# Gate and up as seven block products in three of four feed-forwards, with GpSimd making four weight sums and the low part of two weight blocks

## The chip, the cores and the metric

The kernel runs on one core of a Trainium2 chip. The metric is the device time in microseconds (us) of one execution, as a median over runs; less is better.

## The reference

A trunk of two layers over 512 tokens plus 16 learned meta tokens (L = 528 in all), model width 1024, float32. Each layer is a feed-forward, a mixer (layer 0: gated convolution and a state space; layer 1: windowed attention), and another feed-forward. Only the feed-forwards matter here:

```
def swiglu(x, w_gate, w_up, w_down):
    return (jax.nn.silu(x @ w_gate) * (x @ w_up)) @ w_down

h = h + FFN_RESIDUAL * swiglu(rmsnorm(h, norm_ff1[layer]), ff1_w_gate[layer], ff1_w_up[layer], ff1_w_down[layer])
```

`w_gate` and `w_up` are 1024 x 2816, `w_down` is 2816 x 1024. The first three feed-forwards work on 528 tokens, the last on the 512 real ones.

## The kernel before

Features lie on the 128 partitions, tokens along the free dimension. A float32 product is made as three TensorE passes: each operand is split into a high part (rounded to the fp32r type by ScalarE's copy) and a low part (what is left, by a VectorE subtraction), and the passes are high by high, high weight by low input, low weight by high input. 2816 is 22 blocks of 128.

**Gate and up.** One *unit* is one block of 128 columns of `w_gate` and of `w_up`, all eight blocks of the contraction: 16 weight blocks of 128 x 128, 2048 elements on each partition. SyncE loads a unit into one of two `raw` buffers (`load_unit`, L635), as soon as VectorE has finished the low part of the unit two before it. ScalarE makes `wh` (`split_high`, L1184), VectorE `wl` (`split_low`, L1464), both with two slots. TensorE's `x_job` makes the gate tile in PSUM banks 0 and 1 and the up tile in banks 2 and 3 (`mm3`, L729). For 528 tokens each pass is two matmuls of 264 columns; for the last feed-forward (`REAL`) it is one of 512. So a unit is 16 x 3 x 2 = 96 matmuls of 264 columns, or 48 of 512. VectorE scales the tiles out of PSUM by the norm `r` (`t_a` L1517, `t_c` L1520), ScalarE takes the silu (L1222), VectorE multiplies (L1523), ScalarE makes `act_h` (L1224), VectorE `act_l` (L1525).

**Down.** The 22 blocks of a feed-forward are done in two parts, 12 and 10 (`PART`). After each part eight down tiles follow (`down`), each a sum over the part's blocks: 72 or 60 matmuls. VectorE adds each to `h` (`residual`, L1500). In the last part the next norm's input is made tile by tile (`norm_input`).

Each engine has its own instruction stream in order, and semaphores order them. GpSimd makes state-space tables in the first feed-forward, issues their transfers in the mixer, makes attention's constants right after it, and has nothing at all to do in feed-forwards 1, 2 and 3 (they are counted from 0).

## Time and profile before

| | |
|---|---|
| median of 3 runs | 1954.45 us (1953.42 to 1957.58) |
| the profiled execution, its time | 1953.96 us |
| its span, first to last instruction | 1951.9 us |
| TensorE busy | 1931.4 us, 99% |
| VectorE busy | 967.5 us, 50% |
| ScalarE busy | 605.0 us, 31% |
| GpSimd busy | 315.3 us, 16% |
| mean granted TensorE clock | 0.994 of 2.4 GHz |

The profile gives for each engine its busy time, for groups of equal instructions their count and mean duration, and for a stretch of the timeline each instruction's start, its duration and, in brackets, the idle time before it and what ended it. PE is TensorE, DVE VectorE, ACT ScalarE, POOL GpSimd. Durations of matmuls overlap, so the cost of one is read from how many fit in a stretch.

### The profile page before, as it was taken

How to read it: one execution, taken by the hardware profiler on the slowest of the kernel's cores; microseconds unless marked ns; L12 is line 12 of the kernel's file. 1: busy time of each engine (PE TensorE's matmuls, PEld its weight loads, DVE VectorE, ACT ScalarE, POOL GpSimd, SP SyncE). 2: the span in 40 equal slices, each digit the busy share in tenths (PEclk: the TensorE clock that was granted, in tenths of full speed). 3: DMA queues.
4: the chain of work that ended last, by engine and by line, in shares of the span. 5: the costliest groups of instructions: out<-in, count | busy, mean ns of one | idle time of the engine just before them, and what ended most of it. 6: DMA issues, size and time to landing. Idle time of an engine off the chain costs nothing.

```text
span 1951.9 us, 33853 instructions
## 1 busy us (share of the span) xinstructions
PE 1931.4 (99%) x13943; PEld 1814.2 (93%) x13943; DVE 967.5 (50%) x1059; ACT 605.0 (31%) x710; POOL 315.3 (16%) x568
## 2 busy tenths in 40 slices
PE   7999999999999999999999999999999999999999
PEld 7999999999999999999999999999877778888887
DVE  5443377566665443344564433445555564433443
ACT  5222222332243222222332222223455332222222
POOL 2888888011130000000000000000011000000000
PEclk9999999999999999999999999999999899999999
DMA  6322544354333323432233323322311133233323
GB/s 176 87 81 82 151 134 151 125 128 129 99 84 87 86 82 88 110 87 70 81 108 88 93 83 102 87 70 81 108 44 44 44 104 90 76 96 108 98 71 90
DMA packets 329026, 185.61 MB, mean 95 GB/s; under 512 B 7288, under 2 KB 322968, under 8 KB 328952
## 3 DMA queue, kind: packets, MB, share of 16 engines
q1 hardware_dynamic: 323280, 166.81, 30.6%
q0 software_dynamic: 5344, 17.69, 3.2%
q8 instruction: 53, 0.87, 0.2%
q14 instruction: 21, 0.17, 0.0%
q10 hardware_dynamic: 328, 0.07, 0.0%
HBM read 173.56 MB, written 9.80 MB: 94 GB/s over the span
## 4 chain that ended last, share of the span: by engine, by line
PE 93%; DVE 3%; issue 2%; ACT 2%; ACTq 0%; POOL 0%; DVEq 0%
PE ps L729 77%; PE ps L948 5%; PE ps L990 2%; PE ps L1009 1%; PE ps L1045 1%; PE ps L1173 1%; PE ps L1141 1%; DVE wl L1464 1%; DVE arena L1845 0%; ACT arena L1410 0%; PE ps L770 0%; PE ps L883 0%; PE ps L909 0%; PE ps L908 0%; PE ps L899 0%
## 5 line engine op out<-in xcount | busy, mean ns | idle before, releaser
L729 PE MATMUL ps<-xl,wh 128*128 128x264 f32 (+1 forms) x2448 | 567.1, 301 | 0.0
L729 PE MATMUL ps<-xh,wh 128*128 128x264 f32 (+1 forms) x2448 | 566.1, 301 | 0.7 <-DVE t_a L1517 0.5
L729 PE MATMUL ps<-xh,wl 128*128 128x264 f32 (+1 forms) x2448 | 565.7, 301 | 0.0
L1464 DVE TENSOR_TENSOR wl<-raw,wh 128x2048 fp32r<-128x2048 f32 x173 | 412.8, 2386 | 168.6 <-ACT wh L1184 168.4
L729 PEld LDWEIGHTS ps<-xh,wh 128*128 128x128 f32 x2448 | 392.3, 188 | 18.0 <-DVE t_a L1517 1.1
L1184 ACT ACTIVATE wh<-raw 128x2048 fp32r<-128x2048 f32 x173 | 329.6, 1905 | 246.7 <-PE ps L729 211.2
L729 PEld LDWEIGHTS ps<-xl,wh 128*128 128x128 f32 x2448 | 391.2, 188 | 15.5 <-issue 0.2
L729 PEld LDWEIGHTS ps<-xh,wl 128*128 128x128 f32 x2448 | 391.1, 188 | 15.1
L729 PE MATMUL ps<-act_l,wh 128*128 128x264 f32 (+1 forms) x1232 | 284.7, 301 | 0.0
L729 PE MATMUL ps<-act_h,wh 128*128 128x264 f32 (+1 forms) x1232 | 284.6, 301 | 0.0
L729 PE MATMUL ps<-act_h,wl 128*128 128x264 f32 (+1 forms) x1232 | 284.3, 301 | 0.0
L1520 DVE TENSOR_TENSOR t_c<-ps,r 128x528 f32<-128x528 f32 (+1 forms) x88 | 61.9, 704 | 367.1 <-PE ps L729 367.0
L729 PEld LDWEIGHTS ps<-act_h,wh 128*128 128x128 f32 x1232 | 197.4, 188 | 7.7
L729 PEld LDWEIGHTS ps<-act_l,wh 128*128 128x128 f32 x1232 | 196.8, 188 | 7.4
L729 PEld LDWEIGHTS ps<-act_h,wl 128*128 128x128 f32 x1232 | 196.6, 188 | 7.5
L1224 ACT ACTIVATE act_h<-t_c 128x528 f32 (+3 forms) x88 | 56.5, 642 | 459.7 <-DVE t_c L1523 459.7
L310 POOL TENSOR_TENSOR arena<-arena 128x32 f32<-128x32 f32 (+7 forms) x245 | 186.2, 760 | 24.2 <-DMA ssm_tables<-arena 5.3
L613 POOL TENSOR_SCALAR arena<-arena 128x16 f32<-128x16 f32 x4 | 1.0, 259 | 902.4 <-DVE arena L1833 865.4
L1500 DVE SCALAR_TENSOR_TENSOR h<-ps,h 128x528 f32 (+2 forms) x72 | 50.7, 704 | 192.4 <-PE ps L729 184.2
L1222 ACT ACTIVATE t_bs<-t_a 128x528 f32<-128x528 f32 (+1 forms) x88 | 56.5, 642 | 285.1 <-DVE t_a L1517 285.1
L1525 DVE TENSOR_TENSOR act_l<-t_c,act_h 128x528 f32 (+3 forms) x88 | 70.6, 803 | 78.8 <-ACT act_h L1224 78.8
L1523 DVE TENSOR_TENSOR t_c<-t_c,t_bs 128x528 f32<-128x528 f32 (+1 forms) x88 | 71.0, 806 | 9.0
(296 smaller groups left out, 1686.8 us busy)
## 6 DMA issues: line engine op xcount, KB each, us to landing
raw<-in_ff_w_gate SPq DMA_DIRECT2D x88, 512.0 KB, 4.0
raw<-in_ff_w_up SPq DMA_DIRECT2D x88, 512.0 KB, 5.2
raw<-in_ff_w_down SPq DMA_DIRECT2D x64, 384.0 KB, 4.0
raw<-in_ff_w_down SPq DMA_DIRECT2D x64, 320.0 KB, 3.7
raw<-in_even_w_in SPq DMA_DIRECT2D x16, 512.0 KB, 5.2
raw<-in_attn_w_qkv SPq DMA_DIRECT2D x12, 512.0 KB, 4.6
raw<-in_even_w_out SPq DMA_DIRECT2D x8, 512.0 KB, 4.7
raw<-in_attn_w_o SPq DMA_DIRECT2D x8, 512.0 KB, 4.5
```

Of the source, the lines that this page charges most:

```text
L310: did(g.tensor_tensor(o, x, y, op))
L729: last = nc.tensor.matmul(ps[:, 2 * pair + hf, 0:nh], w[:, slot, b * P:(b + 1) * P], x[:, k0 + k, c0 + hf * nh:c0 + (hf + 1) * nh], start= ...
L948: last = nc.tensor.matmul(ps[:, 2 * (p % 2) + hf, 0:L // 2], w[:, slot, b * P:(b + 1) * P], x[:, k, hf * L // 2:(hf + 1) * L // 2], start= ...
L990: last = nc.tensor.matmul(ps[:, 2 * (d % 2) + hf, 0:L // 2], w[:, slot, b * P:(b + 1) * P], x[:, k, hf * L // 2:(hf + 1) * L // 2], start= ...
L1184: nc.scalar.activation(wh[:, c % 2, :], raw[:, c % 2, :], ACT.Copy).then_inc(wh_ready, 1)
L1222: nc.scalar.activation(t_b[:, cols], t_a[:, cols], ACT.Silu).then_inc(silu_done[n], 1)
L1224: nc.scalar.activation(act_h[:, s + 2 * i, cols], t_c[:, cols], ACT.Copy).then_inc(act_h_done[n], 1)
L1464: v.tensor_tensor(wl[:, c % 2, :], raw[:, c % 2, :], wh[:, c % 2, :].bitcast(F32), ALU.subtract).then_inc(wl_ready, 1)
L1500: v.scalar_tensor_tensor(hd, tile(pair, col), scale, hd, ALU.mult, ALU.add).then_inc(tile_evac, 1)
L1520: v.tensor_tensor(halves(t_c, col), tile(1, col), halves(r, col), ALU.mult).then_inc(tile_evac, 1)
L1523: v.tensor_tensor(t_c[:, cols], t_c[:, cols], t_b[:, cols], ALU.mult).then_inc(gated[n], 1)
L1525: v.tensor_tensor(act_l[:, s + 2 * i, cols], t_c[:, cols], act_h[:, s + 2 * i, cols].bitcast(F32), ALU.subtract).then_inc(act_ready[n], 1)
```

## The change

Feed-forward 0 stays. In feed-forwards 1, 2 and 3 the 22 blocks are done in four parts, 4, 6, 6 and 6, with eight down tiles after each. The first part's four units are as before. The other 18 units each use the Winograd form of Strassen's product: the weights of a unit are seen as 2 x 2 blocks (gate or up by first or second half of the contraction), the inputs as 2 x 2 (half of the contraction by half of the tokens, `first` and `second`), and seven block products take the place of eight. A product is 4 contraction blocks x 3 passes of 264 columns (256 in the last): 12 matmuls, so a unit has 84.

- **GpSimd** makes the three sums of inputs (`t1`, `t2`, `t4`), once for each feed-forward, and for each unit the four weight sums `S1`, `S2`, `S4`, `S3` (512 elements each), and `wl` of `A11`, `A12` (1024 elements, one instruction). The constants for attention now come after its work for feed-forward 2.
- **ScalarE** makes the high parts of the seven forms in five instructions, and copies products 2 and 3 out of PSUM.
- **VectorE** makes the low parts of `A22`, `S1`, `S2` with `S4`, and `S3`, in four instructions, and adds the products up: seven additions of half the tokens each (`t_a` first, `u2`, `w_`, `t_a` second, `u3`, `t_c` first and second). The inputs are scaled by gain and norm beforehand (`scaled_pair`), in the units of the first part.
- **PSUM:** the seven products of a unit take seven of the eight banks, turning by seven from unit to unit. So of a unit's products the first has the free bank, and the second takes the bank of the first product of the unit before, which is read last but one there. There is one set of weight forms (8 x 512 elements, over both slots), so each form is made again when its product has been done.

The core of the diff:

```diff
+    RF = 4
+    PARTS = [RF] + [(NF - RF) // 3] * 3
...
+                    yield part, f, SU * (n - 1) + l, [((3 if part == len(PARTS) - 1 else 4) + 7 * f + x) % 8 for x in range(7)], c
...  GpSimd, seven_tables, once for each unit
+                    pool.wait_ge(raw_landed[c % 2], 32 * (c // 2 + 1))
+                    if sn:
+                        pool.wait_ge(s_lo, 3 * (sn - 1) + 2)
+                    g.tensor_tensor(s1, a21, a22, ALU.add).then_inc(sform, 1)
+                    pool.wait_ge(sform, 4 * sn + 1)
+                    if sn:
+                        pool.wait_ge(s_lo, 3 * (sn - 1) + 3)
+                    g.tensor_tensor(s2, s1, a11, ALU.subtract).then_inc(sform, 1)
+                    pool.wait_ge(sform, 4 * sn + 2)
+                    g.tensor_tensor(s4, a12, s2, ALU.subtract).then_inc(sform, 1)
+                    pool.wait_ge(wl_ready, c)
+                    g.tensor_tensor(s3, a11, a21, ALU.subtract).then_inc(sform, 1)
+                    own = slice(FORM["A11"], FORM["A11"] + 2 * HB)
+                    pool.wait_ge(s_hi, 4 * sn + 3)
+                    g.tensor_tensor(wl_flat[:, own], raw[:, c % 2, 0:2 * HB], wh_flat[:, own].bitcast(F32), ALU.subtract).then_inc(s_own, 1)
...  TensorE: when a bank is free, and a unit
+            def read_out(sn, x):
+                return (copied, 2 * sn + x) if x in (1, 2) else (used, 6 * sn + (6, 0, 0, 1, 2, 3, 5)[x])
...
+                pe.wait_ge(s_lo, 3 * sn + 1)
+                product(0, "A22", table(tf_h, 2), table(tf_l, 2))
+                pe.wait_ge(s_lo, 3 * sn + 2)
+                product(1, "S1", table(tf_h, 0), table(tf_l, 0))
+                pe.wait_ge(s_own, sn + 1)
+                product(2, "A11", half(xh, 0, first), half(xl, 0, first))
+                product(3, "A12", half(xh, XH, first), half(xl, XH, first))
+                pe.wait_ge(s_lo, 3 * sn + 3)
+                product(4, "S2", table(tf_h, 1), table(tf_l, 1))
+                product(5, "S4", half(xh, XH, second), half(xl, XH, second))
+                pe.wait_ge(wl_ready, c + 1)
+                product(6, "S3", half(xh, 0, second), half(xl, 0, second))
...  ScalarE, a unit
+                        if pending is not None:
+                            act_high(*pending)
+                        if nxt:
+                            forms_a(nxt[2], nxt[4], (prod, 7 * sn + 1), (prod, 7 * sn + 2))
+                        for x in (1, 2):
+                            act.wait_ge(prod, 7 * sn + x + 1)
+                            nc.scalar.activation(o_sum[:, sn % 2, x - 1, 0:nh], ps[:, banks_[x], 0:nh], ACT.Copy).then_inc(copied, 1)
+                        if nxt:
+                            forms_b(nxt[2], nxt[4], (prod, 7 * sn + 4))
+                            forms_c(nxt[2], nxt[4], (prod, 7 * sn + 6))
+                        act.wait_ge(used, 6 * sn + 4)
+                        silu(k)
+                        if nxt:
+                            forms_d(nxt[2], nxt[4], (prod, 7 * sn + 7))
...  VectorE, a unit
+                        if nxt:
+                            forms_a(nxt[2], nxt[4])
+                        dve.wait_ge(prod, 7 * sn + 4)
+                        dve.wait_ge(copied, 2 * sn + 2)
+                        v.tensor_tensor(t_a[:, first], p1, bank(3), ALU.add).then_inc(used, 1)
+                        dve.wait_ge(prod, 7 * sn + 5)
+                        v.tensor_tensor(u2, p1, bank(4), ALU.add).then_inc(used, 1)
+                        dve.wait_ge(prod, 7 * sn + 6)
+                        v.tensor_tensor(w_, p5, bank(5), ALU.add).then_inc(used, 1)
+                        dve.wait_ge(used, 6 * sn + 3)
+                        v.tensor_tensor(t_a[:, second], u2, w_, ALU.add).then_inc(used, 1)
+                        if nxt:
+                            forms_c(nxt[2], nxt[4])
+                        dve.wait_ge(prod, 7 * sn + 7)
+                        v.tensor_tensor(u3, u2, bank(6), ALU.add).then_inc(used, 1)
+                        dve.wait_ge(used, 6 * sn + 5)
+                        dve.wait_ge(act_ready[n], k)
+                        v.tensor_tensor(t_c[:, first], u3, bank(0), ALU.add)
+                        v.tensor_tensor(t_c[:, second], u3, p5, ALU.add).then_inc(used, 1)
+                        dve.wait_ge(used, 6 * sn + 6)
+                        dve.wait_ge(silu_done[n], k + 1)
+                        gate(k)
+                        if nxt:
+                            forms_d(nxt[2], nxt[4])
+                        act_low(k, f)
```

On ScalarE `forms_a` is the high parts of `A22` and `S1`, `forms_b` of `A11` with `A12`, `forms_c` of `S2` with `S4`, `forms_d` of `S3`; on VectorE `forms_a`, `forms_c` and `forms_d` are the low parts of the same forms. `prod` counts products, `used` six of the seven additions, `copied` ScalarE's copies. In the first part the first four down tiles also carry `half_high` and `half_low`, the split of the scaled inputs (1056 elements each).

## Rows read from the trace of the kernel before

**Rows 1.** The page: busy times, the chain that ended last, the loads.
```profile
PE 1931.4 (99%) x13943; PEld 1814.2 (93%) x13943; DVE 967.5 (50%) x1059; ACT 605.0 (31%) x710; POOL 315.3 (16%) x568
...
PE ps L729 77%; PE ps L948 5%; PE ps L990 2%; PE ps L1009 1%; PE ps L1045 1%; PE ps L1173 1%; PE ps L1141 1%; DVE wl L1464 1%; DVE arena L1845 0%; ACT arena L1410 0%; PE ps L770 0%; PE ps L883 0%; PE ps L909 0%; PE ps L908 0%; PE ps L899 0%
...
raw<-in_ff_w_up SPq DMA_DIRECT2D x88, 512.0 KB, 5.2
raw<-in_ff_w_down SPq DMA_DIRECT2D x64, 384.0 KB, 4.0
```

**Rows 2.** Windows in feed-forwards 1 and 3: busy time (matmuls), clock, DMA share, GB/s.
```profile
622.40:991.20 368.80, 368.80 (x3018) 368.80 (x3017) 161.59 (x151) 101.94 (x92) 0.00 (x0) 1.00 0.32 88
1600.00:1700.00 100.00, 100.00 (x434) 81.06 (x433) 44.65 (x46) 27.66 (x27) 0.00 (x0) 1.00 0.32 89
```

**Rows 3.** The chain that ended last, one tile of feed-forward 3: start us, us.
```profile
1576.32 5.57 PE ps L729 x24
```

**Rows 4.** VectorE's timeline in feed-forward 1, GpSimd idle: start us, us, instruction.
```profile
739.55 2.29 DVE L1464 TENSOR_TENSOR wl<-raw,wh 128x2048 fp32r<-128x2048 f32 x1 [0.98 <-ACT wh L1184]
741.76 0.70 DVE L1517 TENSOR_TENSOR t_a<-ps,r 128x528 f32<-128x528 f32 x1
747.14 0.71 DVE L1520 TENSOR_TENSOR t_c<-ps,r 128x528 f32<-128x528 f32 x1 [4.68 <-PE ps L729]
747.97 0.71 DVE L1523 TENSOR_TENSOR t_c<-t_c,t_bs 128x528 f32<-128x528 f32 x1
749.61 0.71 DVE L1525 TENSOR_TENSOR act_l<-t_c,act_h 128x528 f32 x1 [0.93 <-ACT act_h L1224]
```

**Rows 5.** VectorE's groups by form: smaller sizes.
```profile
L1523 DVE TENSOR_TENSOR t_c<-t_c,t_bs 128x512 f32<-128x512 f32 x22 | 15.2, 692 | 2.3
L1873 DVE TENSOR_TENSOR act_l<-ps,act_h 128x256 fp32r<-128x256 f32 x16 | 6.8, 425 | 39.6 <-ACT act_h L1420 39.6
L1570 DVE TENSOR_TENSOR wl<-raw,wh 128x1024 fp32r<-128x1024 f32 x1 | 1.2, 1224 | 0.6 <-ACT wh L1270 0.6
```

**Rows 6.** ScalarE's groups by form.
```profile
L1224 ACT ACTIVATE act_h<-t_c 128x512 f32 x18 | 11.4, 632 | 92.0 <-DVE t_c L1523 92.0
L1270 ACT ACTIVATE wh<-raw 128x1024 fp32r<-128x1024 f32 x1 | 1.0, 1038 | 0.0
L1372 ACT ACTIVATE t_bs<-ps 128x256 f32<-128x256 f32 x4 | 1.5, 386 | 3.5 <-PE ps L1009 3.5
```

**Rows 7.** GpSimd's timeline, single instructions with VectorE idle or reading PSUM.
```profile
234.19 1.07 POOL L310 TENSOR_TENSOR arena<-arena 128x512 f32<-128x512 f32 x1
268.94 2.06 POOL L310 TENSOR_TENSOR arena<-arena 128x1024 f32<-128x1024 f32 x1
```

**Rows 8.** Both timelines at 235 us, where both engines read SBUF.
```profile
235.34 3.21 POOL L310 TENSOR_TENSOR arena<-arena 128x512 f32<-128x512 f32 x1
235.05 2.35 DVE L1464 TENSOR_TENSOR wl<-raw,wh 128x2048 fp32r<-128x2048 f32 x1 [1.19 <-ACT wh L1184]
```

**Rows 9.** VectorE's timeline in feed-forward 0 while GpSimd makes tables without pause.
```profile
296.42 4.87 DVE L1464 TENSOR_TENSOR wl<-raw,wh 128x2048 fp32r<-128x2048 f32 x1
301.21 0.70 DVE L1517 TENSOR_TENSOR t_a<-ps,r 128x528 f32<-128x528 f32 x1
303.90 0.71 DVE L1520 TENSOR_TENSOR t_c<-ps,r 128x528 f32<-128x528 f32 x1 [1.99 <-PE ps L729]
304.73 2.02 DVE L1523 TENSOR_TENSOR t_c<-t_c,t_bs 128x528 f32<-128x528 f32 x1
307.70 2.01 DVE L1525 TENSOR_TENSOR act_l<-t_c,act_h 128x528 f32 x1 [0.96 <-ACT act_h L1224]
```

**Rows 10.** All engines at 1588 us: TensorE held until a bank has been read.
```profile
1587.56 0.69 DVE L1517 TENSOR_TENSOR t_a<-ps,r 128x512 f32<-128x512 f32 x1
1588.37 0.19 PEld L729 LDWEIGHTS ps<-xh,wh 128*128 128x128 f32 x1 [0.50 <-issue]
1588.40 0.47 PE L729 MATMUL ps<-xh,wh 128*128 128x512 f32 x1
```

**Rows 11.** GpSimd's timeline after the mixer: the first and last of 16 rows.
```profile
563.25 0.58 POOL L566 DMA_DIRECT2D arena<-in_attn_sinks  x1 [44.07 <-DVE act_l L1739]
...
578.85 1.18 POOL L593 COPY arena<-arena 64x2 f32<-64x2 f32 x4
```

**Rows 12.** Windows in attention (busy time, matmuls, clock) around a drop.
```profile
1480.00:1500.00 20.00, 18.71 (x147) 14.95 (x145) 12.51 (x31) 8.65 (x31) 4.04 (x12) 1.00 0.20 54
1500.00:1510.00 10.00, 8.37 (x69) 6.30 (x68) 5.96 (x20) 6.17 (x19) 3.28 (x15) 0.93 0.00 1
1510.00:1520.00 10.00, 10.00 (x51) 7.03 (x49) 6.61 (x13) 3.59 (x15) 0.00 (x0) 0.50 0.27 79
```

**Rows 13.** TensorE's group by form in the mixer, whose code is written out without loops.
```profile
L948 PE MATMUL ps<-xl,wh 128*128 128x264 f32 x256 | 52.1, 285 | 0.0
```

More of the change, by code:

```diff
@@ new lines, in seven_ffn, with down @@
+            def seven_ffn(n, col):
+                m = FFNORM[n]
+                u0, j = FF[n]
+                for f in range(RF):
+                    x_job(u0 + f, j, 0, (u0 + f) % 2, range(KD), col, m if f == 0 else None)
+                    if f == 0:
+                        token_sums(m, col)
+                    x_job(u0 + f, j + 1, 1, (u0 + f) % 2, range(KD, 2 * KD), col, new_unit=False)
+                    j += 2
+                units = list(seven_units(n))
+                done = 0
+                for part, nf in enumerate(PARTS):
+                    own = [x for x in units if x[0] == part]
+                    for at, (_, f, sn, banks_, c) in enumerate(own):
+                        free = []
+                        for x, bank in enumerate(banks_):
+                            if at == 0:
+                                free.append((tile_evac, j if x > 2 else j - 1) if bank < 4 else (used, 6 * sn) if sn else None)
+                            else:
+                                x_before = own[at - 1][3].index(bank) if bank in own[at - 1][3] else None
+                                if x_before is not None:
+                                    free.append(read_out(sn - 1, x_before))
+                                elif at == 1:
+                                    free.append((tile_evac, j) if bank < 4 else (used, 6 * (sn - 1)) if sn > 1 else None)
+                                else:
+                                    free.append(read_out(sn - 2, own[at - 2][3].index(bank)))
+                        seven(n, sn, banks_, c, col, free)
+                    done += nf
+                    u = own[-1][4] + 1 if own else u0 + RF
+                    flip = 1 if part in (1, 2) else 0
+                    def down(i):
+                        for s in range(2):
+                            pe.wait_ge(wl_ready, u + s + 2 * i + 1)
+                            pe.wait_ge(tile_evac, j + s + 2 * i - 1)
+                            pe.wait_ge(act_ready[n], done - 1)
+                            if own:
+                                pe.wait_ge(used, 6 * own[-1][2] + (6 if s else 2))
+                            mm3((s + flip) % 2, (u + s) % 2, range(nf), act_h, act_l, 0, col,
+                                lambda: pe.wait_ge(act_ready[n], done)).then_inc(tile_full, 1)
+                            if n == 3 and part == 3 and 2 * i + s:
@@ L1242, in ffn @@
-                    if part == 1 and n == 3:
-                        for i in range(KD // 2 - 1):
-                            down(i)
-                        down(KD // 2 - 1, True)
-                    else:
-                        with act.Fori(0, KD // 2) as i:
-                            down(i)
+                            split_high(u0 + s + 1, i, j0 + s + 2 * i)
+                            if part == 1:
+                                norm_input(m + 1, s + 2 * i, col, (tile_evac, j0 + s + 2 * i + 1))
@@ L1534, in ffn, with down @@
                     done += nf
-                    more = m + 1 if part == 1 and n < 3 else None
+                    more = m + 1 if part == 1 else None
                     if more is not None:
                         clear_sums(more)
-                    def down(i, last=False):
+                    def down(i):
                         for s in range(2):
-                            if not (last and s == 1):
-                                split_low(u0 + s + 1, i)
+                            split_low(u0 + s + 1, i)
```

311 lines of the change are left out of this document (277 added, 34 removed).

## The prediction

> **What bounds the kernel now.** I read the page first, for who is busy: TensorE 99% of the span, the others half or less, and the chain that ended last is 77% matmuls of L729, the feed-forwards [rows 1]. Then the windows, for the price of a matmul: 368.8 us hold 3018 of 264 columns, 0.1222 us each, at full clock, and 24 of 512 columns in a row took 5.57 us by the chain, 0.232 each (100 us of that feed-forward hold 434, 0.230) [rows 2, 3]. A unit before is thus 96 x 0.1222 = 11.73 us, in the last feed-forward 48 x 0.232 = 11.13 us. Then the timelines, for how much of that the other engines need. VectorE is through with a unit 3.2 us after it starts to read the up tile (747.14 to 750.32), was idle for 4.68 us before it, and is late for no one [rows 4]. Written-out code runs at the same rate as loops (285 ns, overlapped, in the mixer) [rows 13], so the unrolled streams cost nothing. Fewer matmuls therefore shorten the kernel, as long as nothing else makes TensorE wait. The question is only that.
>
> **What is removed.** 12 matmuls of 96 in 36 units: a unit of 84 is 10.27 us, 1.47 less. In the last feed-forward 84 of 256 columns take the place of 48 of 512. No row has 256 columns; half a 512 is 0.116 us and a 264 is 0.122, so 0.119 with those as ends: 10.0 us a unit, 1.13 less (0.9 to 1.4). The gain with no waiting is 36 x 1.47 + 18 x 1.13 = 73 us. The Trainium skill's page "TensorE: Matmul & The Clock Gate" (Back-to-back issue gap) gives an isolated gap of N/2.4 + 2.5 ns, by which a unit of the last would be an estimated 9.2 us and the interval below 0.6 less; for 264 columns it gives 0.1125 where the row has 0.1222, so the row decides.
>
> **What is added, one unit.** VectorE by size, from 0.425 us at 256, 0.69 at 512, 1.22 at 1024 and 0.71 at 528 [rows 4, 5]: seven half additions at 0.43, low parts 3 x 0.69 + 1.22, gate and `act_l` 2 x 0.71: 7.7 us. ScalarE [rows 6]: three single forms 1.9, two double forms 2.08, two copies 0.8, silu and `act_h` 1.3: 6.1 us. GpSimd with nobody in its way [rows 7]: 4 x 1.07 + 2.06 = 6.3 us. Each fits in 10.27 us. But they don't fit freely.
>
> First, the port. When VectorE's subtraction over two SBUF operands and GpSimd's addition meet, the later one waits: 1.07 becomes 3.21 us when it started 0.29 us behind a 2.35 us subtraction, and that ran at its usual pace [rows 7, 8]. In the other order VectorE pays: 2.29 becomes 4.87, 0.71 becomes 2.0, while the additions with an operand in PSUM stay at 0.70 [rows 4, 9]. So they exclude each other for whole instructions, and this change sets GpSimd's 6.3 us against 5.5 us of such work on VectorE (four low parts, gate, `act_l`, `t_a` second, `t_c` second: 3.3 + 1.4 + 0.86) in each unit: 11.8 us of one resource where TensorE needs 10.27. The page "SBUF — State Buffer" of the Trainium skill (Who interferes with whom) speaks against this change in the same way: a VectorE instruction with two SBUF inputs and a GpSimd one that reads SBUF share a port pair, and the one that comes second blocks until the first has ended. By it the sum is the one below; a reading of the rows by which both merely slow down would give the free-port sum.
>
> Second, the bank. A unit's second product needs the bank that `t_c` first reads and that `t_c` second frees. TensorE has two products, 2.93 us, between the end of product 6 (`S4`) and that second product. VectorE must in this time do, in its order: `w_`, `t_a` second, the low part of `S2`,`S4` (after ScalarE's 1.04 us high part, which itself waits for product 6), `u3`, `t_c` first, `t_c` second. Handing over takes 0.2 us from TensorE, 0.05 to 0.15 between the others, and TensorE restarts 0.12 us after the read [rows 4, 10]; back-to-back instructions overlap by 0.08 (739.55 + 2.29 against 741.76) [rows 4]. Without the port, from product 6: high part 0.2 to 1.25, low part 1.3 to 2.52, `u3` to 2.87, `t_c` first 2.99 to 3.42, second to 3.77, TensorE at 3.9: 1.0 us late. With it: GpSimd's `A11`,`A12` began when their high part was done (product 4, which ended 2.93 before, + 0.2 + 1.04 + 0.08) and ends at 0.45; its `S1` for the unit after runs 0.53 to 1.6. `t_a` second asks at 0.73 and gets 1.6 to 2.03, the low part 2.0 to 3.2, `u3` to 3.55, `t_c` first 3.67 to 4.1. GpSimd's `S2` waited for the low part and runs 3.28 to 4.35, so `t_c` second is 4.35 to 4.78, and TensorE starts at 4.9.
>
> The interval from unit to unit is then 5 products (60 x 0.1222 = 7.33) + 4.9 = 12.2 us, in the last feed-forward 60 x 0.119 + 4.9 = 12.0. That is above the 11.73 and 11.13 of a plain unit. Each part of six has five such intervals, and its last unit runs through in 10.27 (10.0), as nothing is behind it. Feed-forwards 1 and 2: 30 x 12.2 + 6 x 10.27 = 427.6 against 36 x 11.73 = 422.3, +5. The last: 15 x 12.0 + 3 x 10.0 = 210 against 200.3, +10. VectorE is blocked some 3.2 us a unit (behind `S1`, `S2`, `S4`, `S3`), 7.7 + 3.2 = 10.9, inside 12.2. Loads: 1 MB in 12.2 us is the rate of now (88 GB/s, [rows 2]), and 5.2 us to land [rows 1] leaves them early. So 15 us are lost in the units.
>
> **What the shorter parts cost.** Before, 12 or 10 blocks a down tile (8.8 us, 72 x 0.1222) hid every hand-over. Now 4 blocks are 2.93 us, 6 are 4.4 us.
> - Last seven-product unit to down, 9 times: `u3`, `t_c`, gate, `act_h`, `act_l` end at 0.2 + 1.3 + 0.1 + 0.7 + 0.8 + 0.8 = 3.95, wanted at 5/6 of 4.4 = 3.67; behind them the second tile's weights (0.84 + 0.96) come 0.4 late. 0.8 each: 7 us.
> - Part of four to down, 3 times: `act_l` at 3.4, wanted at 3/4 of 2.93 = 2.2: 1.3 each, 4 us.
> - First seven-product unit behind the four-block tiles, 3 times: its load starts when the seventh tile's weights are split, takes 5.2, then four sums and `A11`,`A12` on GpSimd (6.3 + 0.4 + some 0.7 blocked). Counted from the end of the seventh tile the load has landed at 1.2 and the low part of `A11`,`A12` is there at 8.6; TensorE wants it after the eighth tile and two products, at 5.9. 2.7 each, 8 us.
> - The scaling and tables in units two to four: 8 operations of 0.75 and 4 low parts of 0.98 on VectorE before the gate tile is read. Before, VectorE had 5 us free a unit; now the third unit's gate read is some 2.7 us late: 8 us over three.
> - End of feed-forwards 1 and 2: behind the seventh `norm_input` come the whole next unit's high and low part (1.9 + 2.3), under a tile of 4.4 in place of 7.3 us: 2.3 late each, 5 us.
> Attention's constants (17 us of GpSimd, 563.25 to 580.03) [rows 11] fit under the last eight down tiles (35 us), before attention: nothing. Bounds of these five: 15 us (the hand-overs that come within 1 us of their time all in time) to 50 (each another 1 us later, over 18 places); I take 32.
>
> **The sum.** 5 + 10 + 32 = 47 us on the profiled 1953.96 (0.5 under the median): 2001 us. Without the port the same sum is 45 x 1.0 less for the units and about 4 for the transitions.
>
> **Rivals.**
> - *The port costs nothing on this chain* (GpSimd's `S1` happens to fall elsewhere, or it yields): intervals 11.2 and 11.0, 2001 - 49 = 1952, no change. Against it: 0.71 becomes 2.02 [rows 4, 9]. Chance 0.08.
> - *TensorE is never held at the bank* (other side): units at 10.27 and 10.0, -73 + 28 = -45: 1909 us. It needs the step from product 6 to the freed bank to take under 2.93 us. For: VectorE is only 75% busy. Against: the serial sum is 3.9 even with a free port. Chance 0.09.
> - *VectorE and GpSimd serialise wholly*: if all five GpSimd instructions fall on VectorE's path, a unit is 7.7 + 6.3 = 14.0: 45 x 1.9 = 86 more, 2087 us. For: 296 to 308 us, where every SBUF operation waited about as long as a GpSimd one [rows 7, 9]. Against: 2.2 us of PSUM additions and the waits leave room. It decides once VectorE's idle time in a unit (1.3 us in mine) is gone. Chance 0.12.
> - *The clock falls*: TensorE would pause 2 us in every 12. In attention, where it was busy 8.4 of 10 us with short matmuls, the granted clock then fell to 0.50, 1.2 GHz [rows 12]. If two products a unit ran at half rate, 45 x 2.9 = 132 more: 2133. Against: for 20 us before, busy 18.7 of 20, it kept 1.00 [rows 12]. The Trainium skill's page "TensorE: Matmul & The Clock Gate" (HAM oscillation) describes such falls in kernels that wait again and again; the rows here show one fall. Chance 0.07.
>
> **The numbers.** My forecast, 2001 us, has 0.64, with its own range of 1980 to 2030. The 8-in-10 range runs from the free port (1952) to short of full serialisation: 1950 to 2065. From the cases, and 0.2% (4 us) being what a measurement can tell: faster 0.09 + a third of the free port + a little of mine = 0.13; the same 0.05; slower 0.82.
>
> **What would show it.** TensorE idle once in nearly every seven-product unit, before its second product, released by VectorE's `t_c` second, about 2 us; fewer and no shorter matmuls but a longer span; `t_a` second and `t_c` second well above 0.43 us, gate and `act_l` above 1 us, while `t_a` first, `w_`, `u3` and `t_c` first stay at 0.43. Wrong if unit intervals are near 10.3 us, if the wait sits at the weight forms instead, or if the clock row in feed-forwards 1 to 3 is below 1.

## The result and the profile after

The changed kernel takes 2083.2 us (median of 4 runs, 2078.3 to 2091.0), the kernel before 1956.0 us beside it: a ratio of 1.066 [1.062, 1.070], slower. The forecast was 2001, its range 1950 to 2065: the sign was right, the size was not, by 82 us. The profiled execution took 2086.6 us against 1954.0, 132.7 more. Of a later run, e_reads, one execution, the profiled one, took 6354.8 us where the other four took 2002 to 2011; its time leaves that one out, and no line of its trace is used.

The page's busy times and its row of the granted clock, by 40 slices:

```profile
PE 1932.0 (93%) x14159; PEld 1836.2 (88%) x14159; DVE 1328.3 (64%) x1635; ACT 744.1 (36%) x1106; POOL 806.6 (39%) x886
...
PEclk9999999999999999999999998989999999999989
```

TensorE is as busy as before (1931.4, [rows 1]), though its products take some 73 us less work, and it is idle for 152.8 us of the span against 20.5. So both halves need an explanation: the 132 us of new idle time, and where the 73 us of saved matmuls went. The mean granted clock answers for the second: 0.961 against 0.994. Lost are (1 - 0.961) x 2084.8 = 81 us of full clock, before (1 - 0.994) x 1951.9 = 12. Where they are lost the windows show (start:end, length, busy time, then the clock, DMA share, GB/s): feed-forwards 1 and 2, attention, feed-forward 3, before and after:

```profile
600.00:1385.00 785.00, 785.00 (x6400) 782.88 (x6399) 354.06 (x328) 225.80 (x207) 0.00 (x0) 1.00 0.32 89
1385.00:1575.00 190.00, 184.28 (x1100) 144.33 (x1098) 107.55 (x261) 88.55 (x225) 19.48 (x76) 0.96 0.20 54
1575.00:1950.00 375.00, 373.18 (x1624) 301.83 (x1622) 161.87 (x148) 104.68 (x94) 0.00 (x0) 1.00 0.33 91
...
640.00:1465.00 825.00, 741.63 (x5638) 730.02 (x5637) 570.29 (x687) 302.88 (x455) 336.81 (x234) 0.94 0.30 82
1465.00:1655.00 190.00, 181.66 (x1100) 141.95 (x1098) 106.78 (x259) 87.79 (x225) 19.41 (x76) 0.97 0.20 56
1655.00:2080.00 425.00, 378.65 (x2270) 338.44 (x2269) 284.76 (x339) 151.05 (x226) 162.28 (x106) 0.94 0.29 81
```

Added up over windows of 5 us, the three changed feed-forwards lose 74 us of full clock, where they lost none before, and attention 5 in place of 9. None of the runs below edits attention, and its loss is anything from 5 to 17 us there, so a run's mean clock isn't a measure of what its feed-forwards do; their own loss is given where it matters.

TensorE's waits (us in total, times, longest):

```profile
PE ps L903 <- DVE t_c L1920: 96.0, 45, 4.4
PE ps L903 <- POOL wl L631: 14.9, 7, 4.0
PE ps L801 <- DVE t_a L1883: 8.2, 3, 3.1
...
PE ps L801 <- DVE wl L1732: 3.9, 8, 1.9
...
PE ps L801 <- DVE act_l L1855: 2.3, 3, 0.8
```

The first row is the wait that the prediction named: 45 times, before the second product (L903 is the first pass of a product), released by the second `t_c` addition (L1920). VectorE's timeline across one interval of feed-forward 1 (start, us, instruction):

```profile
708.21 0.41 DVE L1906 TENSOR_TENSOR t_a<-arena,ps 128x264 f32<-128x264 f32 x1
...
710.99 0.46 DVE L1912 TENSOR_TENSOR t_a<-arena 128x264 f32<-128x264 f32 x1
711.67 2.04 DVE L1820 TENSOR_TENSOR wl<-arena,wh 128x1024 fp32r<-128x1024 f32 x1 [0.23 <-ACT wh L1411]
713.64 0.42 DVE L1916 TENSOR_TENSOR arena<-arena,ps 128x264 f32<-128x264 f32 x1
714.09 0.43 DVE L1919 TENSOR_TENSOR t_c<-arena,ps 128x264 f32<-128x264 f32 x1
714.43 0.98 DVE L1920 TENSOR_TENSOR t_c<-arena 128x264 f32<-128x264 f32 x1
715.44 1.68 DVE L1851 TENSOR_TENSOR t_c<-t_c,t_bs 128x528 f32<-128x528 f32 x1
...
717.84 1.84 DVE L1855 TENSOR_TENSOR act_l<-t_c,act_h 128x528 fp32r<-128x528 f32 x1
```

GpSimd's in the same stretch:

```profile
708.76 2.40 POOL L631 TENSOR_TENSOR wl<-raw,wh 128x1024 fp32r<-128x1024 f32 x1 [2.25 <-ACT wh L1411]
711.11 1.51 POOL L620 TENSOR_TENSOR arena<-raw 128x512 f32<-128x512 f32 x1
713.86 1.26 POOL L624 TENSOR_TENSOR arena<-arena,raw 128x512 f32<-128x512 f32 x1 [1.23 <-DVE wl L1820]
715.20 1.37 POOL L626 TENSOR_TENSOR arena<-raw,arena 128x512 f32<-128x512 f32 x1
717.81 1.31 POOL L628 TENSOR_TENSOR arena<-raw 128x512 f32<-128x512 f32 x1 [1.25 <-DVE wl L1820]
```

L620, L624, L626 and L628 are `S1`, `S2`, `S4` and `S3`. Read the two timelines against each other. `t_c` second waits for `S2` (713.86 + 1.26): 0.98 where it takes 0.43 alone. The gate (L1851) waits for `S4` (1.68 for 0.71), and `act_l` for `S3` (1.84 for 0.71). Additions with an operand in PSUM stay at 0.41 to 0.43. The low part of `S2`,`S4` is at 2.04 because `S1`, which follows `A11`,`A12` (L631), ran until 712.62.

The windows of the first and third of three intervals in a row (the third is cut 0.3 us short) and of 100 us:

```profile
702.95:715.56 12.61, 10.46 (x85) 10.28 (x85) 10.70 (x14) 5.43 (x9) 7.81 (x6) 1.00 0.30 83
...
728.14:742.00 13.86, 12.01 (x84) 11.80 (x84) 10.51 (x13) 5.53 (x9) 7.55 (x6) 0.88 0.28 77
800.00:900.00 100.00, 88.98 (x660) 87.61 (x659) 71.74 (x87) 36.11 (x57) 45.12 (x27) 0.91 0.25 70
```

An interval is 12.6 us at full clock, and longer where the clock falls. The chain that ended last shows how, in matmuls of 264 columns at the head of that third interval:

```profile
728.74 0.12 PE ps L903
728.87 0.12 PE ps L904
728.99 0.21 PE ps L905
729.20 0.22 PE ps L903
...
732.06 0.22 PE ps L904
```

TensorE stood for 2.2 us, restarted at 728.14 at 0.12 us a matmul (2.4 GHz), and from 728.99 to 732.46 was granted the lower level, 1.2 GHz: 16 matmuls at 0.22. Then it went on at 0.12. That costs 1.5 us, and that interval was 14.1 us (by the starts of `t_a` first, L1906). Of the 45 intervals 34 are above 13 us, 23 of them between 13.8 and 15, and the mean is 13.35.

### The profile page after: what moved, and what is told of

It is laid out like the page before. It is cut to its first block, busy times and chain, and to the rows that moved or that the text cites. A ratio compares the mean times of both kernels' runs of the same rounds, so it can differ in the third digit from the quotient of the medians.

```text
span 2084.8 us, 35756 instructions
## 1 busy us (share of the span) xinstructions
PE 1932.0 (93%) x14159; PEld 1836.2 (88%) x14159; DVE 1328.3 (64%) x1635; ACT 744.1 (36%) x1106; POOL 806.6 (39%) x886
## 4 chain that ended last, share of the span: by engine, by line
PE 56%; issue 23%; DVE 9%; POOL 6%; ACT 5%; ACTq 0%; DMA 0%; SPq 0%; POOLq 0%; DVEq 0%
PE ps L801 26%; PE ps L903 6%; PE ps L904 5%; PE ps L905 5%; PE ps L1111 5%; PE ps L1153 2%; POOL wl L631 2%; ACT wh L1411 2%; DVE t_c L1920 2%; DVE wl L1820 2%; PE ps L1172 1%; PE ps L1208 1%; POOL arena L620 1%; PE ps L1336 1%; DVE wl L1732 1%
## 5 line engine op out<-in xcount | busy, mean ns | idle before, releaser
L1732 DVE TENSOR_TENSOR wl<-raw,wh 128x768 fp32r<-128x768 f32 (+2 forms) x167 | 262.8, 1574 | 98.3 <-ACT wh L1347 97.7
L1347 ACT ACTIVATE wh<-raw 128x768 fp32r<-128x768 f32 (+2 forms) x167 | 210.8, 1262 | 229.7 <-PE ps L801 192.4
L903 PE MATMUL ps<-act_h,wh 128*128 128x264 f32 (+1 forms) x648 | 200.4, 309 | 98.0 <-DVE t_c L1920 96.0
L801 PE MATMUL ps<-act_h,wh 128*128 128x264 f32 (+1 forms) x1232 | 286.7, 302 | 4.6 <-DVE act_l L1855 2.3
L801 PE MATMUL ps<-act_l,wh 128*128 128x264 f32 (+1 forms) x1232 | 284.1, 300 | 0.0
L801 PE MATMUL ps<-act_h,wl 128*128 128x264 f32 (+1 forms) x1232 | 283.7, 300 | 0.0
L903 PE MATMUL ps<-xh,wh 128*128 128x264 f32 (+1 forms) x864 | 260.2, 301 | 15.2 <-POOL wl L631 14.9
L904 PE MATMUL ps<-xl,wh 128*128 128x264 f32 (+1 forms) x864 | 257.2, 298 | 0.0
L905 PE MATMUL ps<-xh,wl 128*128 128x264 f32 (+1 forms) x864 | 255.9, 296 | 0.0
L1820 DVE TENSOR_TENSOR wl<-arena,wh 128x512 fp32r<-128x512 f32 x162 | 219.2, 1356 | 25.9 <-ACT wh L1411 16.1
L903 PEld LDWEIGHTS ps<-act_h,wh 128*128 128x128 f32 x648 | 133.6, 206 | 107.6 <-issue 104.1
L801 PE MATMUL ps<-xl,wh 128*128 128x264 f32 (+1 forms) x1008 | 219.5, 294 | 0.0
L801 PE MATMUL ps<-xh,wl 128*128 128x264 f32 (+1 forms) x1008 | 219.1, 294 | 0.0
L620 POOL TENSOR_TENSOR arena<-raw 128x512 f32<-128x512 f32 x54 | 86.1, 1595 | 341.7 <-DMA raw<-in_ff_w_up 281.3
L801 PEld LDWEIGHTS ps<-act_h,wh 128*128 128x128 f32 x1232 | 196.9, 188 | 16.8 <-issue 4.4
L905 PE MATMUL ps<-act_h,wl 128*128 128x264 f32 (+1 forms) x648 | 197.1, 304 | 0.0
L904 PE MATMUL ps<-act_l,wh 128*128 128x264 f32 (+1 forms) x648 | 196.4, 303 | 0.0
```

Of the source, the lines that this page charges most:

```text
L620: g.tensor_tensor(s1, a21, a22, ALU.add).then_inc(sform, 1)
L801: last = nc.tensor.matmul(ps[:, 2 * pair + hf, 0:nh], w[:, slot, b * P:(b + 1) * P], x[:, k0 + k, c0 + hf * nh:c0 + (hf + 1) * nh], start= ...
L903: nc.tensor.matmul(ps[:, banks_[x], 0:nh], wh_flat[:, at], x_h[k], start=(k == 0), stop=False)
L904: nc.tensor.matmul(ps[:, banks_[x], 0:nh], wh_flat[:, at], x_l[k], start=False, stop=False)
L905: last = nc.tensor.matmul(ps[:, banks_[x], 0:nh], wl_flat[:, at], x_h[k], start=False, stop=(k == XH - 1))
L1347: nc.scalar.activation(wh[:, c % 2, 0:width], raw[:, c % 2, 0:width], ACT.Copy).then_inc(wh_ready, 1)
```

## Experiments

"The first addition" is `t_c` first (L1919), which is the last reader of the bank that the next unit's second product needs. "Own" is GpSimd's low part of `A11`,`A12` (L631). An interval is from the start of `t_a` first in one unit to that of the next; a part has five.

**GpSimd's reads taken away (e_memset).** The five instructions keep their place, waits and signals, but write constants. The sums of weights and the low part of `A11`,`A12` are left out here.

```diff
-g.tensor_tensor(s1, a21, a22, ALU.add).then_inc(sform, 1)
+g.memset(s1, 0.01).then_inc(sform, 1)
...  s2, s4, s3 in the same way
-g.tensor_tensor(wl_flat[:, own], raw[:, c % 2, 0:2 * HB], wh_flat[:, own].bitcast(F32), ALU.subtract).then_inc(s_own, 1)
+g.memset(wl_flat[:, own].bitcast(F32), 0.0).then_inc(s_own, 1)
```

> The changed kernel in its own order, with GpSimd's five instructions of a unit writing constants and reading nothing (weight sums and the low part of `A11`, `A12` left out). It prices the port within the chain from product 6 to the bank. Theory: the chain is 3.9 us as worked out with a free port, not 5.3, the interval 11.2 us; 45 x 1.3 = 60 us, 15 us of waits for GpSimd, some 40 of the clock: about 1965 us (1950 to 1985), still slower or the same as before, since the bank holds TensorE 1.0 us a unit. Rival, the port is all of it: near 1907 us, as with the other order.

Measured: 1952.3 us, 0.998 [0.996, 0.999] of the kernel before; clock 0.992. VectorE's timeline for the same instructions:

```profile
714.88 1.23 DVE L1820 TENSOR_TENSOR wl<-arena,wh 128x1024 fp32r<-128x1024 f32 x1 [0.26 <-ACT wh L1411]
716.02 0.42 DVE L1916 TENSOR_TENSOR arena<-arena,ps 128x264 f32<-128x264 f32 x1
716.48 0.43 DVE L1919 TENSOR_TENSOR t_c<-arena,ps 128x264 f32<-128x264 f32 x1
716.82 0.43 DVE L1920 TENSOR_TENSOR t_c<-arena 128x264 f32<-128x264 f32 x1
717.29 0.71 DVE L1851 TENSOR_TENSOR t_c<-t_c,t_bs 128x528 f32<-128x528 f32 x1
...
718.71 0.71 DVE L1855 TENSOR_TENSOR act_l<-t_c,act_h 128x528 fp32r<-128x528 f32 x1
```

and GpSimd's, beside `t_c` second and beside `act_l`:

```profile
716.80 0.52 POOL L626 MEMSET arena<- 128x512 f32 x1
718.65 0.53 POOL L628 MEMSET arena<- 128x512 f32 x1 [1.33 <-DVE wl L1820]
```

Every duration is back at its price alone. The constants also take GpSimd half the time, but no step of the chain to the bank waits for a signal of GpSimd's in either trace; what became shorter is the low part of `S2`,`S4` (2.04 to 1.23) and `t_c` second (0.98 to 0.43), 1.36 us together, and the interval at full clock went from 12.61 to 11.25, 1.36 us too. So the blocked time of VectorE is all of that difference. Most intervals are 11.25 us, in the last feed-forward 11.0: the prediction's free-port figures were 11.2 and 11.0, and its free-port sum 1952. So the chain without contention was read rightly. The changed kernel takes 131 us more than this run and 127 more than the kernel before: its whole loss hangs on GpSimd's five instructions. It divides by place: 45 intervals x (13.35 - 11.28) = 93 us; the six passages from part to part within a feed-forward, 48.4 instead of 45.2 (47.4 instead of 43.4 in the last), 21 us; and 19 us in the three stretches that end with a feed-forward's first seven-product unit. Together 133, the difference of the two profiled executions. TensorE still waits at the bank 45 times, but 0.8 us each (36.6 in all, none over 0.9), and there the clock stays up: the three feed-forwards lose 5 us of full clock, not 74.

**The pauses filled (e_fill).** 16 matmuls that nobody reads, into the bank of the third product, ahead of the second product of all but a part's first unit. If only idle time counted, this would change nothing or cost something; if the pauses bring the clock down, it gives time back.

```diff
                 pe.wait_ge(s_lo, 3 * sn + 2)
+                if sn % 6:
+                    pe.wait_ge(*free[2])
+                    for k in range(16):
+                        at = slice(FORM["S1"] + k % XH * P, FORM["S1"] + (k % XH + 1) * P)
+                        nc.tensor.matmul(ps[:, banks_[2], 0:nh], wh_flat[:, at], tf_h[:, 0, k % XH, 0:nh], start=(k == 0), stop=(k == 15))
                 product(1, "S1", table(tf_h, 0), table(tf_l, 0))
```

> 16 matmuls whose result nobody uses are put before each held product (into the bank of product 3, which overwrites it), so that TensorE works in the pause. Everything else is as in the changed kernel; the output is the same. Theory that the pauses make the clock fall: the clock's mean goes from 0.961 to about 0.99, intervals stay at 12.6 us and none are 14: 2083 - 66 = about 2017 us (2000 to 2035). Rival, the clock falls for another reason or its falls cost little: 2075 to 2095 us.

Measured: 2041.7 us, 1.043 [1.040, 1.046]; 41.5 us less than the changed kernel, with 720 matmuls more, but above the 2035 us that was expected at most. Clock 0.984. The window that had 0.91, then the three stretches as above:

```profile
800.00:900.00 100.00, 97.66 (x793) 96.58 (x792) 73.66 (x89) 35.68 (x57) 45.43 (x26) 1.00 0.28 79
...
600.00:1435.00 835.00, 804.51 (x6444) 794.25 (x6443) 597.92 (x713) 316.40 (x471) 354.84 (x242) 0.99 0.30 84
1435.00:1630.00 195.00, 189.05 (x1098) 147.48 (x1097) 106.29 (x259) 87.48 (x223) 19.46 (x76) 0.93 0.20 54
1630.00:2035.00 405.00, 388.42 (x2517) 349.32 (x2515) 286.35 (x341) 150.53 (x227) 172.86 (x106) 0.99 0.31 85
```

The intervals are at most 12.66 us but for each feed-forward's first (13.2), and none is 14; the mean is 12.20. The feed-forwards now lose 13 us of full clock in place of 74, and attention, which isn't touched, lost 14 in this execution in place of 5. Work without use made the kernel 2% faster: that the pauses cost clock is shown. The 41.5 us are a net figure and not the clock's alone: the added matmuls have a cost, attention took 9 us back, and eight intervals are near 11.5 us, below the 12.6 of full clock. In the one of these that was looked at (820 to 832 us) `S1` came late, behind its load, and didn't block the low part of `S2`,`S4` (1.21).

**The bank freed earlier (e_first).** The bank is signalled by the first addition, its last reader, instead of by the second.

```diff
+return (bank0, sn + 1) if x == 0 else ...
-v.tensor_tensor(t_c[:, first], u3, bank(0), ALU.add)
+v.tensor_tensor(t_c[:, first], u3, bank(0), ALU.add).then_inc(bank0, 1)
```

> The bank of a unit's first product is handed back by `t_c` first, which reads it, and no longer by `t_c` second. Theory of the bank (the pause ends with the chain from product 6 to that bank, and the clock falls because of the pause): the chain loses 0.35 us of overlap up to the whole 0.98 us of `t_c` second, the pause goes from 2.1 to 1.2 to 1.7 us, 45 intervals give 18 to 40 us, and the falls of the clock get fewer (0 to 66 us more): 1975 to 2065 us. Rival, VectorE and GpSimd as a whole set the unit (their port is full): the wait only moves elsewhere and the time stays above 2070 us.

Measured: 2041.7 us, 1.043 [1.040, 1.046]; clock 0.971, the mean interval 12.25, and the wait at the bank 72.3 us. The intervals became 1.1 us shorter on the mean (49 us), the kernel 41.5; attention lost 9 us more of full clock in the profiled execution than in the changed kernel's, which is about the difference.

**Readings before the weights (e_reads, and e_both with the earlier signal).** VectorE makes the low part of `S2`,`S4` behind the gate instead of ahead of `u3`.

```diff
-                        if nxt:
-                            forms_c(nxt[2], nxt[4])
                         dve.wait_ge(prod, 7 * sn + 7)
...
                         gate(k)
                         if nxt:
+                            forms_c(nxt[2], nxt[4])
                             forms_d(nxt[2], nxt[4])
```

> The changed kernel with one edit, VectorE's readings before the low part of `S2` with `S4`; the bank still comes with `t_c` second. Theory of the full port: VectorE is busy all the time in the run with both edits (11.6 us a unit), so the second edit can matter little on top of the order: 1998 to 2015 us. Rival, the chain to the bank is what counts, the two edits add up: 2083 - 42 for the other edit and the same again for this, and this one alone near 2041 us.

> As the run before, and VectorE reads product 7 and makes `t_c` and the gate first, and only then the low part of `S2` with `S4`. Theory of the bank: nothing long stands between product 7 and the freed bank, so no pause there; the interval falls from 12.6 us to what VectorE needs with its blocked time, about 10.9, 45 x 1.7 = 76 us, and the clock stays up, 66 us: about 1940 us (1920 to 1970). Rival, the port is full: 11.8 us a unit at least, a new wait at the forms, 2083 - 36 - some of the clock: 1990 to 2050 us.

Measured: e_reads 2003.9 us, 1.025 [1.022, 1.028]; e_both 1999.2 us, 1.020 [1.018, 1.023], clock 0.981. The two edits don't add up: the order is worth 79 us alone, the signal 41.5 alone and 5 on top of the order. For e_both 1940 us (1920 to 1970) was expected, and its rival, the full port, came true: it stops at steady intervals of 11.63 where the bank is free early. VectorE's timeline there:

```profile
713.90 1.82 DVE L1820 TENSOR_TENSOR wl<-arena,wh 128x1024 fp32r<-128x1024 f32 x2
715.64 1.79 DVE L1855 TENSOR_TENSOR act_l<-t_c,act_h 128x528 fp32r<-128x528 f32 x1
717.35 1.79 DVE L1820 TENSOR_TENSOR wl<-raw,wh 128x512 fp32r<-128x512 f32 x1
719.07 1.80 DVE L1820 TENSOR_TENSOR wl<-arena,wh 128x512 fp32r<-128x512 f32 x1
```

and GpSimd's:

```profile
715.26 1.60 POOL L624 TENSOR_TENSOR arena<-arena,raw 128x512 f32<-128x512 f32 x1 [2.32 <-DVE wl L1820]
716.94 1.66 POOL L626 TENSOR_TENSOR arena<-raw,arena 128x512 f32<-128x512 f32 x1
718.56 1.76 POOL L628 TENSOR_TENSOR arena<-raw 128x512 f32<-128x512 f32 x1
```

VectorE is now busy 39.59 of 40 us (710 to 750) and is itself the limit. With both queues full the engines take turns, one instruction each: 0.7 of VectorE's own and 1.1 of GpSimd's make 1.8, three times in a row (the last three rows; the first one is two low parts merged, 1.82 also where GpSimd reads nothing). Here GpSimd's sums cost VectorE more (1.1 each) than it would need to make them itself (0.69 at 512, [rows 5]). The rival "serialise wholly" names this state, in part: the PSUM additions still go ahead beside GpSimd. What e_both would be if GpSimd read nothing is e_both_memset, which leaves out what e_memset leaves out:

> The run with the first two edits, and GpSimd's five instructions of a unit write constants (memset) and read nothing: the weight sums and the low part of `A11` and `A12` are left out. Same waits, same bytes for everybody else. Theory of the port: a GpSimd instruction that reads nothing doesn't hold VectorE up; VectorE needs 7.7 us, TensorE is the limit at 10.27: 1999 - 45 x 1.3 - 14 - clock 20 = about 1905 us (1890 to 1925). Rival, VectorE's instructions are slow by themselves in this order: above 1980 us.

Measured: 1907.0 us, 0.973 [0.971, 0.976], no wait at the bank at all, steady intervals of 10.22 and 9.86 us. This is the prediction's "never held" (10.27 and 10.0, 1909 us). 9.86 / 84 is 0.1174 us for a matmul of 256 columns, where 0.119 was taken.

**`A11`,`A12` by VectorE (e_vlow alone; e_all with e_both and the table low parts after the gate tile's reading).**

```diff
+                own = slice(FORM["A11"], FORM["A11"] + 2 * HB)
+                dve.wait_ge(s_hi, 4 * sn + 3)
+                v.tensor_tensor(wl_flat[:, own], raw[:, c % 2, 0:2 * HB], wh_flat[:, own].bitcast(F32), ALU.subtract).then_inc(s_own, 1)
...  called behind u2; taken out of GpSimd's stream
```

> The changed kernel, with the low part of `A11` and `A12` made by VectorE behind `u2` and no longer by GpSimd; all else as changed. Theory of the bank with the port: the chain from product 6 is the same (GpSimd's `S1` for the unit after can now start earlier and be out of the way of `t_a` second and of the low part of `S2` with `S4`, up to 0.8 us a unit); also the 14.9 us of waits for GpSimd's low part go: 2083 - 15 - (0 to 36) = 2030 to 2068 us. Rival, GpSimd's time is what sets the unit (8.3 us busy of 12.6): 3.4 us a unit less, under 1990 us.

> Four edits together: the bank handed back by `t_c` first, VectorE's readings before the low part of `S2` with `S4`, the low part of `A11` and `A12` by VectorE, and the low parts of the input tables after the gate tile has been read. The run with the first two had a unit of 11.6 us in which VectorE was busy 9.9 of 10 us, its SBUF work and GpSimd's one after the other. Theory of the full port: 2.14 us of GpSimd go from that row and 1.14 of VectorE come in, 10.6 us a unit, 45 x 1.0 less, 8 + 14 us of other waits less, and some of the clock: 1999 - 45 - 22 - 10 = about 1922 us (1905 to 1950), faster than the kernel before. Rival, VectorE itself is the limit and not the port: 1.1 us a unit more, about 2030 us.

Measured: e_vlow 2052.9 us, 1.049 [1.046, 1.051]: 30 us less than the changed kernel, where the waits for L631 were 14.9 in all; the wait at the bank is about as long (91.2). The clock went from 0.961 to 0.969, some 16 to 19 us of such a span (24 us less lost in the feed-forwards, 5 more in attention), which is about the rest; no run takes the two apart. e_all 1996.5 us, 1.019 [1.017, 1.022], against an expected 1922: a miss. Its steady interval is 12.05, longer than in e_both. VectorE is back to back already, and the low part costs it 1.13 more. In return it is blocked for only 0.7 less: `t_a` second waited 1.07 behind GpSimd's low part and `t_c` second 0.30 behind `S1`, and now `t_a` second waits 0.66 behind `S1`. The difference, 0.4, is what the interval grew by.

**The weight sums by VectorE, own left to GpSimd (e_vsums, then e_vsums_late).** With the order of e_both and the later table low parts.

```diff
+                v.tensor_tensor(s1, a21, a22, ALU.add).then_inc(sform, 1)
+                v.tensor_tensor(s2, s1, a11, ALU.subtract).then_inc(sform, 1)
+                v.tensor_tensor(s4, a12, s2, ALU.subtract).then_inc(sform, 1)
+                v.tensor_tensor(s3, a11, a21, ALU.subtract).then_inc(sform, 1)
...  e_vsums_late only, ahead of GpSimd's own
+                    pool.wait_ge(s_lo, 3 * sn + 2)
```

> The bank handed back by `t_c` first, VectorE's readings before the low part of `S2` with `S4`, the input tables' low parts after the gate tile's reading; and the four weight sums of a unit made by VectorE (4 x 0.61 us in a row) and not by GpSimd, which keeps the low part of `A11` and `A12` alone. Theory of the port: in the runs before, each of GpSimd's four sums held a VectorE instruction up by 1.1 us, more than the 0.61 that VectorE needs for the sum itself; the low part of `A11`, `A12` lay under VectorE's three PSUM additions. VectorE's unit is 11.6 - 4.4 + 2.5 = 9.7 us, TensorE's 10.27 is the limit: close to the run whose GpSimd only writes constants (1907 us), with 0.7 us a unit of waits left: 1905 to 1935 us, faster than the kernel before. Rival, VectorE is the limit whoever makes the sums: 11 us a unit or more, 1970 us or more.

> The run whose weight sums VectorE makes, with one more wait: GpSimd starts the low part of `A11` and `A12` only when VectorE has made that of `S1`. In that run they met: `S1`'s low part took 2.9 us in place of 0.68 and VectorE's unit was 11.8 us. Theory of the port: behind that wait the 2.1 us of GpSimd lie under VectorE's three PSUM additions (1.1 us) and hold up `t_a` second by 0.9; VectorE's unit is 11.8 - 2.2 + 0.9 = 10.5 us; 45 x 1.2 = 54 us less, some of the 24 us of first-unit waits and some clock less: about 1935 us (1920 to 1955), faster than the kernel before by 1%. Rival, another limit lies just under 11.8 us: above 1975 us.

Measured: e_vsums 1999.1 us, 1.022 [1.019, 1.024], a miss. Two lines of its VectorE timeline say why:

```profile
702.00 0.69 DVE L1822 TENSOR_TENSOR wl<-raw,wh 128x512 fp32r<-128x512 f32 x1
702.60 2.89 DVE L1822 TENSOR_TENSOR wl<-arena,wh 128x512 fp32r<-128x512 f32 x1
```

GpSimd's own (702.27, 2.66 us) gets in ahead of the low part of `S1`. It now has one instruction a unit, and it falls in the wrong place. One wait more, until that low part is done, moves it under the PSUM additions: e_vsums_late took 1949.0 us, 0.995 [0.993, 0.996], clock 0.992. Now it blocks `t_a` second (1.79 for 0.43) in place of the low part of `S1` (2.89 for 0.69): 0.85 us less a unit, and the steady interval went from 11.81 to 10.95. The place of a single GpSimd instruction was worth 50 us.

**All of a unit's vector work on VectorE (e_vector).** GpSimd makes only the sums of inputs.

> The same run with nothing left of a unit on GpSimd: VectorE makes the weight sums and all low parts (GpSimd keeps the three input sums of each feed-forward). Theory: 7.7 + 2.5 + 1.14 less 0.08 for each instruction that follows another, 10.7 us a unit without any instruction held up; about 1940 us (1925 to 1960). It tells how much GpSimd brings in this place at all: if the run above is no faster, nothing. Rival, as above: above 1975 us.

Measured: 1933.4 us, 0.986 [0.984, 0.988]; 1.4% faster than the kernel before. VectorE's timeline, where the four sums and the 1024-wide low part stand at their own price:

```profile
708.26 0.69 DVE L1810 TENSOR_TENSOR arena<-arena,raw 128x512 f32<-128x512 f32 x1
708.98 0.69 DVE L1812 TENSOR_TENSOR arena<-raw,arena 128x512 f32<-128x512 f32 x1
...
712.08 1.21 DVE L1831 TENSOR_TENSOR wl<-raw,wh 128x1024 fp32r<-128x1024 f32 x1
```

The steady interval is 10.72 (10.27 would be TensorE's own), the wait at the bank 11.7 us in 36 places. Of the 150 us from 2083 to 1933, the signal and the order brought 84 (e_both). The other 66 came from taking work away from an engine with idle time and giving it to the busiest of the three that serve TensorE, together with the later table low parts, which no run tries alone (TensorE waits 5.1 us less for `t_a`, 4.0 more for `act_l`).

**The short parts alone (e_short, e_short_narrow).** The kernel before with parts of 4, 6, 6 and 6 in all four feed-forwards; in the second the splits for down tiles are as wide as the part's blocks.

```diff
-PART = [12, NF - 12]
+PART = [4, 6, 6, 6]
...  e_short_narrow, both splits of down weights
-wl[:, c % 2, :], raw[:, c % 2, :], wh[:, c % 2, :]
+wl[:, c % 2, 0:width], raw[:, c % 2, 0:width], wh[:, c % 2, 0:width]
```

> The kernel before with parts of 4, 6, 6 and 6 blocks in all four feed-forwards, all units plain: what the shorter parts cost by themselves. By my terms: 4 x 1.3 for the part of four, 12 x 0.8 for the parts of six, 3 x 2.3 for the ends, together 22 us: 1978 us (1965 to 1990). Rival, the hand-overs are hidden: within 4 us of 1956.

> The kernel before with parts of 4, 6, 6 and 6 blocks in all four feed-forwards and plain units, and with the split of a down tile's weights only as wide as the part (512 or 768 elements), as the changed kernel has it. In the run before with the same parts every down tile still split 2048 elements, 1.9 + 2.3 us under a tile of 2.9 or 4.4. My terms: 4 x 1.3 + 12 x 0.8 + 3 x 2.3 = 22 us: 1978 us (1968 to 1990). Rival, short parts cost far more than that: over 2000 us.

Measured: e_short 2118.7 us, 1.081 [1.078, 1.084], far above the 1990 expected at most, and it prices more than the parts: its splits stayed 2048 wide (some 2.3 us) under tiles of 2.9 and 4.4 us, and TensorE waited for them 70 times, 106.7 us. e_short_narrow 1997.1 us, 1.020 [1.018, 1.023]: about 9.5 us for each feed-forward, mostly 18.5 us of waits for down weights and 4.7 for `act_l`. Expected were 22 us over all four (1968 to 1990 us), so it is a miss too, by nearly a factor of two; in it the first part's tables are not made and units are whole, so it prices the parts of a plain kernel.

## Why the prediction was right in direction and wrong in size

**Right.** *The bank.* "A unit's second product needs the bank that `t_c` first reads and that `t_c` second frees": 45 waits, at that place, by that releaser, 96.0 us against 45 x 1.97 = 89 forecast. *The port.* The gate and `act_l` above 1 us, `t_c` second above 0.43 and the additions with an operand in PSUM at 0.43 came out as forecast, and e_memset removed all of it. One instruction was named wrongly: `t_a` second stayed at 0.46, and the low part of `S2`,`S4` was blocked in its place (2.04). *What the matmuls save.* With no holding, 10.22 and 9.86 for 10.27 and 10.0. *The free-port sum.* 1952 forecast; e_memset 1952.3. The match to the microsecond is luck: e_memset also removes the 8 us of GpSimd's late low part, so about 8 us elsewhere were missed. *The short parts.* The waits that the prediction listed add up to 14.9 + 8.2 + 3.9 + 2.3 = 29 us against 32: GpSimd's late `A11`,`A12` at 14.9 in all instead of 8, the gate tile's reading 8.2 as forecast, the hand-overs and the ends 6.2 instead of 16. So the sum is near because two of its terms were off in opposite directions.

**Wrong: "The clock falls", chance 0.07, counted with 0 in the sum.** The argument against it was one window in attention where TensorE, busy 18.7 of 20 us, kept 1.00 [rows 12]. That window bounds short pauses. Of a pause of 2 us in each 12 it says nothing, and the forecast itself set 45 of these. The same rows have the drop to 0.50 right behind a window with idle time in it (busy 8.4 of 10 us), and the forecast's own intervals all had idle time. The trace has 0.961, 70 us of full clock more lost than before, 74 in the three feed-forwards less 4 in attention; filling the pauses (e_fill) brings the 74 down to 13 and the time down by 41.5, and pauses of 0.8 us (e_memset) lose 5. The rival's price (two products of a unit at half rate, 2.9 us, in each interval) was too high: 1.5 us for the stretch of 16 matmuls shown, and 74 / 45 = 1.6 us an interval on the mean. The Trainium skill's page "TensorE: Matmul & The Clock Gate" (A second HAM failure mode: psum-queue depth-cycling) describes another kernel with this trouble: TensorE idles briefly between groups of matmuls, often, and the clock falls again and again, a price beyond the idle time. The trace agrees, with 0.88 over one interval and 0.91 over 100 us; the forecast cited the section ahead of it, and gave the case 0.07 on the strength of one window.

**Wrong in size: "TensorE at 4.9".** It was 5.28 us from the end of product 6 (710.28, which is 702.95 + 60 x 0.1222) to 715.56. `A11`,`A12` took 2.40, not 2.06, and ended at +0.9 instead of +0.45. So `t_a` second got through at once, and `S1`, now later and 1.51 long, held up the low part of `S2`,`S4` instead, which ended at +3.4 instead of +3.2. `S2` behind it took 1.26, not 1.07, and `t_c` second ended at +5.1. That is 0.4 us an interval, up to 18 us in all. GpSimd's prices from [rows 7], 2.06 and 1.07, were too low for these instructions: the low part took 2.40, the greater part of it beside a VectorE that reads PSUM, and never less in any of the 54 units, nor in e_vsums_late. Why stays open.

Clock and chain, 70 + 18 = 88 us, stand about even with the 86 us that the profiled execution lies above the forecast (132.7 - 47).

**The rivals.** "Serialise wholly" gave 2087 us, and that the changed kernel came out there is chance: in it VectorE is busy 10.7 of 12.6 us, so it isn't the limit. It becomes so as soon as the bank is free early (e_both), at the point that the prediction gave: when VectorE's idle time in a unit is gone. "Never held" was out of reach for the order as written, as the serial sum of 3.9 us said.

## What to carry to other kernels

Before giving VectorE's work to an idle GpSimd, count its two-input SBUF instructions in the same stretch: with both queues full each GpSimd instruction costs VectorE its whole length, so the hand-over only pays where GpSimd's work falls under VectorE's PSUM additions or idle time. A pause that recurs every few microseconds on TensorE has a second price, the clock; shorten it first, and until then treat the clock as a term of the sum and not as a remote case. Free a PSUM bank with the instruction that reads it last: here that one signal was worth 41 us alone. Before that, look at what stands in the reader's queue ahead of the reading: moving one low part behind it was worth 79 us, and then the signal only 5.
